# The first step of an MLP's down phase: ScalarE and VectorE take the returned operands ahead of the last pair's parts, and the load queue takes one weight block ahead of two operands

## The reference

```python
def sq_relu_mlp(h, w1, w2):
    return jnp.square(jax.nn.relu(h @ w1)) @ w2      # w1: 1024 x 4096, w2: 4096 x 1024
# per layer, after the mixer and the attention:
f = sq_relu_mlp(rms_norm(h, mlp_pre_g[i]), mlp_w1[i], mlp_w2[i])
h = h + rms_norm(f, mlp_post_g[i])
```

## Time and profile before

| | |
|---|---|
| median of three runs | 3032.22 us (3029.85 to 3036.36) |
| profiled execution: time, span | 3032.02 us, 3030.1 us |
| mean granted TensorE clock | 0.993 of full speed |
| busy: TensorE, VectorE, ScalarE, GpSimd | 2964.2, 2112.5, 1443.0, 826.5 us |
| matmuls in the trace | 16926 |
| step 0 of the down phase begins (product a1) | 1032.50 us in layer 0 |

### The profile page before, as it was taken

How to read it: one execution, slowest core, us unless ns; L and a number is a source line. 1 busy time by engine, 2 the same in 40 slices (tenths; PEclk the granted TensorE clock), 3 DMA queues, 4 the chain that set the end, 5 groups by cost and what they waited for, 6 DMA issues and landing times.

```text
span 3030.1 us, 44749 instructions
## 1 busy us (share of the span) xinstructions
PE 2964.2 (98%) x16926; PEld 2420.1 (80%) x16926; DVE 2112.5 (70%) x2910; ACT 1443.0 (48%) x2648; POOL 826.5 (27%) x804
## 2 busy tenths in 40 slices
PE   8999999999999999999999999999999999999997
PEld 6788888887888778887888788878888788877886
DVE  8275638547788867778977666644754778886776
ACT  3345545335777621225433566644534667762112
POOL 3529400000466633330000112100000066663332
PEclk9999999999999999999999999999999999999999
DMA  6730241002566786533444323123101356687653
GB/s 206 232 114 24 98 125 56 29 28 100 208 245 241 267 326 240 206 120 134 142 147 153 102 60 111 56 70 112 42 29 35 139 198 246 243 298 271 250 209 125
DMA packets 198560, 457.33 MB, mean 151 GB/s; under 512 B 13792, under 2 KB 71408, under 8 KB 196464
## 3 DMA queue, kind: packets, MB, share of 16 engines
q1 hardware_dynamic: 159552, 415.11, 38.9%
q10 hardware_dynamic: 38832, 39.85, 3.9%
HBM read 304.96 MB, written 149.95 MB: 150 GB/s over the span
## 4 chain that ended last, share of the span: by engine, by line
PE 82%; DVE 10%; ACT 3%; DMA 2%; issue 2%; POOL 1%; ACTq 0%; DVEq 0%; SPq 0%; POOLq 0%
PE ps L3319 21%; PE ps L3541 10%; PE ps L3542 10%; PE ps L3543 10%; PE ps L3335 6%; PE ps L3773 3%; PE ps L3774 3%; PE ps L3775 3%; PE ps L3808 2%; PE ps L3702 2%; PE ps L3391 1%; DVE work L2135 1%; DMA wraw<-wstream_dram 1%; DVE work L2151 1%; DVE hres L2166 1%
## 5 line engine op out<-in xcount | busy, mean ns | idle before, releaser
L3319 PE MATMUL ps<-act,whi 128*128 128x512 f32 x2384 | 751.6, 396 | 5.6 <-DVE work L2286 2.7
L3319 PEld LDWEIGHTS ps<-act,whi 128*128 128x128 f32 x2384 | 444.2, 188 | 115.1 <-issue 13.9
L3319 PE MATMUL ps<-act,wlo 128*128 128x512 f32 x1192 | 466.8, 392 | 0.0
L2119 DVE TENSOR_TENSOR wlo<-wraw,whi 128x1024 fp32r<-128x1024 f32 x255 | 320.8, 1260 | 203.3 <-ACT whi L1132 170.4
L1017 POOL TENSOR_TENSOR stagedf<-quads 128x1024 f32<-128x1024 f32 x28 | 73.4, 2623 | 1062.3 <-ACTq L1423 1062.3
L2584 DVE TENSOR_TENSOR work<-work,ps 128x512 f32<-128x512 f32 x360 | 240.4, 683 | 137.7 <-PE ps L3543 136.1
L1484 ACT ACTIVATE whi<-wraw 128x1024 fp32r<-128x1024 f32 x112 | 115.8, 1056 | 380.0 <-POOL wraw L1036 316.4
L3319 PEld LDWEIGHTS ps<-act,wlo 128*128 128x128 f32 x1192 | 223.8, 188 | 49.3
L3541 PE MATMUL ps<-act,whi 128*128 128x512 f32 x624 | 246.9, 396 | 1.1 <-DVE work L2584 1.1
L3543 PE MATMUL ps<-act,wlo 128*128 128x512 f32 x624 | 244.8, 392 | 0.0
L1132 ACT ACTIVATE whi<-wraw 128x1024 fp32r<-128x1024 f32 x124 | 130.3, 1056 | 156.8 <-DMA wraw<-wstream_dram 153.8
(11 more groups left out here) (432 smaller groups left out, 7183.7 us busy)
## 6 DMA issues: line engine op xcount, KB each, us to landing
wraw<-wstream_dram SPq DMA_DIRECT2D x248, 512.0 KB, 3.6
hid_store<-staged SPq DMA_DIRECT2D x168, 512.0 KB, 3.4
act<-hid_store SPq DMA_DIRECT2D x36, 1024.0 KB, 11.2
hresr<-hid_store SPq DMA_DIRECT2D x56, 512.0 KB, 10.8
qkvz<-work ACTq DMA_DIRECT2D x32, 512.0 KB, 2.8
work<-qkvz ACTq DMA_DIRECT2D x64, 256.0 KB, 3.3
act<-hid_store SPq DMA_DIRECT2D x30, 512.0 KB, 11.3
presum<-wstream_dram SPq DMA_DIRECT2D x48, 256.0 KB, 4.2
```

The costliest lines, as they stand in the source:

```text
L2119: TT(wlo[s][:], wraw[s][:], whi[s][:].bitcast(F32), ALU.subtract).then_inc(w_split, 1)
L3319: last = mm(out_of(u)[:, 0:width], (wlo if hl else whi)[s][:, at:at + P], rhs(kt, xp, e), start=kt == hl == xp == 0, stop=kt == kts - 1 an ...
```

## The change

Three things are done, in each layer's MLP.

1. ScalarE (from the end of the last q): `raw_hi` of B22, T3 and T4 each come before parts of pair 13 that stood ahead of them. Parts T13, T2, T4 of pair 13 move behind the copies a1, a5, b1, b5 and a6, and ahead of b6. `down_hi(0, 2)` is taken apart: the block ahead of the copy b6, its sums behind it.
2. VectorE: the sums of block (0, 1) are split at the end of the last q, no longer within the start of step 0. `raw_lo("B22")` goes ahead of part B21. Parts T13, T2, T4 move behind k = 9, where the block (0, 2) is split first. The sums of that block follow at k = 12.
3. SP: in every step i up to 4, `load` of the next step's block j = 2 goes ahead of operands B11 and T1 of step i + 2.

`TOUCHED` is written out by hand. It has the same eight names in the same order as the expression that it replaces.

```diff
-TOUCHED = tuple(name for name in PRODUCTS if name[0] in "ab" and name[1] in FIRST_TOUCH)
+TOUCHED = ("a1", "a5", "b1", "b5", "a6", "b6", "a4", "b4")
@@ SP
                     more = i + 2 < MLP_G - 1
+                    load(n + MLP_T * i + 6)
                     if more:
                         operand(i + 2, "B11")
                         operand(i + 2, "T1")
-                    load(n + MLP_T * i + 6)
-                    if more:
                         operand(i + 2, "T2")
@@ ScalarE
                 raw_hi("T2")
+                raw_hi("B22")
                 part_hi(PAIRS + 1, "B21")
                 first_copy("a1")
-                raw_hi("B22")
-                part_hi(PAIRS + 1, "T13")
                 raw_hi("T3")
                 first_copy("a5")
-                part_hi(PAIRS + 1, "T2")
                 raw_hi("T4")
                 first_copy("b1")
+                first_copy("b5")
+                first_copy("a6")
+                part_hi(PAIRS + 1, "T13")
+                part_hi(PAIRS + 1, "T2")
                 part_hi(PAIRS + 1, "T4")
-                first_copy("b5")
-                down_hi(0, 2)
-                first_copy("a6")
+                block_hi(nd + 2, prep_no(layer, None, 0, 2))
                 first_copy("b6")
+                sums_hi(prep_no(layer, None, 0, 2), sums_of(None, 2))
                 first_copy("a4")
                 down_hi(0, 3)
                 first_copy("b4")
@@ VectorE, end of q
                     if more:
                         part_of_sums_lo(x, bufs, 0, "24")
+                    else:
+                        sums_lo(prep_no(layer, None, 0, 1), sums_of(None, 1))
                     part_lo(q + 2, "B22")
@@ VectorE, down phase
                         raw_lo("T2")
+                        raw_lo("B22")
                         part_lo(PAIRS + 1, "B21")
-                        sums_lo(prep_no(layer, None, 0, 1), sums_of(None, 1))
-                        raw_lo("B22")
-                        part_lo(PAIRS + 1, "T13")
                         raw_lo("T3")
                     eng.wait_ge(evac, down_unit(layer, i, "a1"))
                     for k in range(len(PRODUCTS)):
                         add(i, k)
-                        if i == 0 and k == 3:
-                            part_lo(PAIRS + 1, "T2")
                         if i == 0 and k == 5:
-                            part_lo(PAIRS + 1, "T4")
                             raw_lo("T4")
-                        if k == (5 if i else 9):
+                        if i == 0 and k == 9:
+                            block_lo(nd + 2, prep_no(layer, None, 0, 2))
+                            for op in ("T13", "T2", "T4"):
+                                part_lo(PAIRS + 1, op)
+                        if i == 0 and k == 12:
+                            sums_lo(prep_no(layer, None, 0, 2), sums_of(None, 2))
+                        if i and k == 5:
                             down_lo(i, 2)
                         if k == 14:
                             down_lo(i, 3)
```

## The result

The changed kernel takes 3038.64 us in the median of 20 runs, and the kernel before 3033.57 in the median of 20 beside it. The ratio is 1.0018 (95% interval 1.0012 to 1.0024), or 3.6 to 7.3 us more. One of the 20 took 11453 us, which leaves the median where it is. The forecast was 6.3 less. The profiled spans are 3037.5 and 3030.1 us. Single runs of this kernel spread over 10 us, so beside the ratio I give a second measure for every kernel: **D**, the time from the last matmul of the up phase's sums to the last of the down phase, of both layers together. It is 571.6 us before (286.8 and 284.8) and 578.6 after (290.2 and 288.4), 7.0 more.

A forecast was written before the change was run, and what follows sets the result against it. TensorE, busy 2964.2 of 3030.1 us, was taken as the bound. Layer 0 gains 0 + 4.1 and layer 1 0.3 + 1.9, together 6.3 us less: 3025.9 from the median, range 3021 to 3030.5.

The forecast's parts named there:

- a3's 3.3 us: Step 0, layer 0: TensorE's 3.29 us wait at a3 goes, with a3 beginning at 1042.8 instead of 1045.87.
- forecast 0.4, 0.8, 1.0: Step 0, layer 0: new small delays at a6 (0.35 us), b6 (0.8) and a4 (0.95) from ScalarE's new order.
- the 3.4 forecast: Step 0, layer 0: a4 comes 3.4 us ahead of the kernel before; only 0.9 of it is left after c7.
- the 1.74 assumed: VectorE's raw_lo B22 beside GpSimd lasts 1.74 us, from 1040.4 to 1042.1.
- the rival's 2.8: Rival: raw_lo B22 is held up by GpSimd's sum, lasting 2.8 us; 4.3 us less in total, 3027.9; chance 0.14.
- c7 waits for VectorE's read of c6: Step 0: a new 2.5 us stall at c7, behind GpSimd's block (0, 3); c7 begins at 1063.9 in layer 0.
- its landing at 1081 to 1082: Block (1, 2), loaded ahead of 2.1 MB, lands 5.4 us sooner; a7's wait in step 1 goes, 4.1 and 1.9 us.
- GpSimd's `down_prep(0, 3)` starts 3.0 us later: Step 0, layer 0: T4's part ends at 1053.65 and GpSimd starts block (0, 3) 3.0 us later, at 1056.65.
- The rival "slower": T4's store meets a busy queue, lands after 9.3 us; c7 at 1070.3, both layers 12.8 against 6.3, 3038.7; chance 0.06.
- the term of 1.5 us: Behind c7's 2.5 us stall TensorE's clock drops for a stretch, costing 1.5 us.
- In later steps there is no wait of TensorE's to gain: Later steps of the down phase: no TensorE wait to gain; the sum holds no term for them.
- the queue starts 1 us sooner: Step 1's loads: the queue starts 1 us sooner, so block (1, 3), asked 4.1 us earlier, is just met.

The follow-up runs named there:

- e6: Changed kernel with one more wait on SP: step 1's loads go out only once pair 13's stores have landed; 3041.87 against 3032.60 us, ratio 1.0026.
- e4: Changed kernel with pair 13's parts spread out again on ScalarE and VectorE, and the load moved in step 0 only; 3027.89 against 3033.34 us, ratio 0.9981.
- e10: Kernel before, with operands B11, T1 and B21 of step 1 issued ahead of pair 13's late stores; 3031.55 against 3033.01 us, ratio 0.9996.
- e7: Kernel before, with SP's new load order in steps 1 to 4 alone; 3038.17 against 3032.60 us, ratio 1.0015.
- e2: Changed kernel with SP's old load order, so only the engines' order is new; 3033.68 against 3033.34 us, ratio 1.0004.
- e5: Changed kernel with block (0, 3)'s sums in other memory, so GpSimd waits for no store; 3038.26 against 3032.60 us, ratio 1.0022.
- e12: e4 with the edits of e5 and e10 added; 3022.71 against 3033.01 us for the kernel before, ratio 0.9962.

## Why the prediction was wrong

**Right.** a3's 3.3 us went, for waits of 0.4, 0.5 and 0.7 at a6, b6 and a4 in layer 0 (forecast 0.4, 0.8, 1.0). Up to a4 layer 0 lost 2.7 us after and 5.9 before (beyond 0.23 us a matmul): 3.3 gained of the 3.4 forecast. `raw_lo` B22 lasted 2.13 us beside GpSimd in layer 0 and 2.32 in layer 1, more than the 1.74 assumed and less than the rival's 2.8, and a3 did not wait for it. c7 waits for VectorE's read of c6, behind GpSimd's block (0, 3), behind the store. Block (1, 2) was at GpSimd at 1083.87, where I had its landing at 1081 to 1082, and a7 of step 1 waits no more.

**The step that failed** is "Today T4 ends at 1050.97, and GpSimd's `down_prep(0, 3)` starts 3.0 us later, on the landing. New: 1056.65." I carried a store's landing time from a place where the queue was nearly empty to one where it was the fourth of a burst, 2 MB, with loads right behind. It measured 6.84 us; e6 splits the excess into 2.9 for the burst and 1.0 for the loads, and e4 and e10 move it to 4.5 and 8.5 by spreading the stores or filling the queue. The rival "slower" named this link and this kind of cause, but at 9.3 us, and I gave it 0.06 on the ground that "the queue is empty". It was, until the burst itself filled it. That this rival's time, 3038.7, is the measured one is luck: it had c7 at 1070.3, where it came at 1068.37, and nothing at d4.

**The clock behind it** was the term of 1.5 us; with a wait of 6 us it was 2.5 in each layer. Wait and stretch together cost c7 4.9 and 4.7 us more than forecast.

**"In later steps there is no wait of TensorE's to gain"** was taken as a cost of nothing. Seven new waits at d4, each making the gap 0.55 us longer, are 3.8 us (e7 shows them on the kernel before, and e2 without SP's edit has one of the seven and 3.3 less of D).

Together these are 4.9 + 4.7 + 3.8 = 13.4. With the forecast's -6.3 that is +7.1, and D rose by 6.97; the median of the runs rose by 5.1.

**A term that I had with the wrong sign** without its changing the sum: for step 1's loads, "the queue starts 1 us sooner". Block (1, 0) was issued 0.75 us later and landed 3.2 later (0.45 of each is the later frame). c7's long wait hid it. It explains why mending c7 alone (e5) gained nothing, and why both of my expectations there failed. Block (1, 2) too was issued only at 1076.58, behind c7's wait, and not by 1071.1.

**Where e5 and e6 lose it again.** In D, e5 is 3.0 us worse than the changed kernel itself, and e6 1.4. e5 saves 8.9 us at c7 in each layer. From c4 to the end of step 0 it loses 3.6 and 4.0 against the changed kernel, in step 1 5.6 and 5.7, in steps 2 to 6 0.1 and 1.7. TensorE is at c7 6.5 us sooner, and block (1, 0) lands 1.5 us later (1063.58). e6 saves 1.7 and 2.8 us at c7 and loses 3.5 and 3.4 in step 1.

**Open.** Why this comes to a little more than what was saved isn't shown; in the medians e5 and the changed kernel are level (+5.7 and +5.1). For e7 D rose by 1.5 and the median by 5.6 (interval 1.8 to 7.6). In its profile 4.6 of the 6.7 us that the span is longer lie ahead of layer 0's down phase, where its edit does nothing; what makes them is not known.

## What to carry to other kernels

When producers are moved together, their stores go out together: price the last one's landing by the bytes ahead of it in the burst and by what is issued right behind, not by how long such a store takes alone. Look also at what stands behind the stores in the same issuing queue, for it starts late by the same amount, and at the idle time that the queue gets ahead of them, which transfers that are needed anyway can fill (4.9 us of D here with the engines' order untouched, together with the sums' place and one load moved; alone, in e10, it delayed the stores and brought nothing clear of the spread). A transfer that comes sooner is not free either: it moves GpSimd's work next to VectorE's.

## What the runs showed of the hardware

- A 0.5 MB store issued by SP into an empty queue took 2.6 us to land in most of these traces, and 3.2 in layer 0 of the changed kernel. In a burst each further one landed 1.2 to 1.4 us behind the one ahead, and the last 2.3 to 2.6 with loads right behind it, 1.3 to 1.7 without (e6). In a queue full of loads it took 8.4 us (e10). The Trainium skill ("DMA: Bandwidth & Descriptors", Anatomy of one DMA) gives, for a DMA issued by GpSimd, some 2.0 us fixed and the bytes at 436 GB/s, an estimate of 3.2 us for this size. SP's stores here are at that or up to 0.6 under it.
- SP's own issue of a transfer took 0.3 us with the queue empty and up to 3.6 us with it full (an operand at 1066.10 in the changed kernel).
- The slow stretch does not go by the wait alone. Behind 6 us of idle TensorE twelve or thirteen matmuls began at 1.2 GHz. Behind a gap of 2.50 us in layer 1 of e4 there was none, and behind gaps of 2.28 us (layer 0 of e10) and 2.39 (layer 1 of e12) there was one. Behind 3.24 us in layer 1 of e10 it was the longest of all, fourteen matmuls. Windows of e4, of both layers of e10, and of e12, right behind these waits (columns as in the earlier trace rows):

```profile
2714.30:2718.00 3.70, 3.60 (x15) 2.93 (x16) 3.13 (x5) 2.00 (x3) 2.84 (x5) 1.00 1.05 394
...
1065.40:1069.20 3.80, 3.78 (x10) 3.00 (x11) 2.04 (x4) 2.90 (x5) 2.74 (x4) 0.55 1.05 391
2718.20:2724.70 6.50, 6.43 (x16) 5.04 (x17) 4.57 (x8) 2.94 (x5) 2.80 (x4) 0.52 1.05 397
...
2698.30:2701.40 3.10, 3.10 (x9) 2.37 (x8) 1.76 (x3) 1.96 (x3) 0.00 (x0) 0.51 1.03 419
```
